# Two-layer hybrid encoder: inner matrices without a zero fill, queries and keys copied out ahead of the rotary, first scan tables and lambda factors moved

## The chip, the cores and the metric

One core of a Trainium2 chip. The metric is the device time of one execution in microseconds. TensorE (PE) multiplies, VectorE (DVE), ScalarE (ACT) and GpSimd (POOL) do the elementwise work, SyncE (SP) issues most transfers. Matmul results stand in PSUM, eight banks of 128 partitions by 512 floats; GpSimd works on SBUF only.

## The reference

```python
for layer in range(2):
    xn = rms_norm(x, norm_mix[layer]);  proj = xn @ w_in[layer]        # 256 x 1024 @ 1024 x 4096
    q, k, v, u, gates = split(proj)                                     # 512, 512, 512, 512, 2048 columns
    q, k = rotary(q), rotary(k)                                         # x1*cos - x2*sin, x2*cos + x1*sin
    lam = exp(sum(lp[0]*lp[1])) - exp(sum(lp[2]*lp[3])) + lam_init
    a = rms_norm(diff_attention(q, k, v, lam), attn_subln) * (1 - lam_init)
    s = gelu(s5_bidirectional(u, ...))                                  # complex diagonal scan, both directions
    s = s * sigmoid(s @ w_glu[layer])
    x = x + (g0 * (a @ w_branch[0]) + g1 * (s @ w_branch[1])) @ w_out[layer]
    x = x + (swiglu if layer == 0 else top-2-of-8 expert swiglu)(rms_norm(x, norm_ffn[layer]))
return rms_norm(x, norm_final)
```

The batch is 1, the sequence 256 tokens, the width 1024. All is in float32.

## The kernel before

Each large product is computed from split operands: ScalarE copies a 128 x 2048 tile of weights to `hi` (rounded, L1175), VectorE computes `lo` as the rest (L1568), and TensorE adds three products per 128 rows (L641, `three`). A layer's mixer has 25 such tiles, t + 0 to t + 24. The input projection takes tiles 0 to 15, two per group of 512 columns, in the order u, v, q, k and four gate groups; the four gate groups are interleaved with the attention and scan loop of eight turns. The 256 tokens are two halves `th`, each with its own accumulation bank `PJ[th]`.

The order of the work is written out by hand for every engine, with semaphores between them; there is no scheduler. The parts around the change:

- **Rotary** (VectorE, `rotary`). It waits for tiles 4 and 5 (queries) or 6 and 7 (keys), and per half multiplies `PJ[th]` with the cosines (L1621) and with the sines in two 256-wide pieces (L1624), both scaled by the inverse norm in the same operation, into the scratch `areg`. Then it releases the bank and adds both (L1629) to `qk`. In layer 0 the query rotary stands between `input_power(3)` and the split of tile 7, the key rotary before the splits of tiles 8 and 9.
- **Inner matrices** (TensorE, `inner`). A first matmul per bank writes 448 columns of zeros over the whole bank `PY` (the identity against a column of zeros), and then the diagonal `kdiag` and the 16-row products of `bbar` and `cblk` accumulate on it. ScalarE copies the result to `kc` (L1276), and SyncE moves pieces of it to `cbm` in 16 transfers (`inner_moves`, L554).
- **B transposed** (TensorE and ScalarE). Eight turns of transposes through two banks, evacuated by ScalarE (L1213) in the order 6, 7, 0, 1, 2, 3, 4, 5. After the turn g == 1 ScalarE makes the scan tables of turn 0 (`scan_tables(l, 0)`: L1284, then L1290), which wait for GpSimd's phase products (`wtab_half`, L2166 and L2167).
- **GpSimd** (layer 0): powers of C (`c_chain`, L430 to L436), phasors (L451 to L472), phase products (L410, L2166, L2167), then one `turn_forward` per turn (L2185 to L2192), whose states TensorE takes in `s5_out`. In layer 1 the powers and phasors are made long before.
- **VectorE before the loop**: `rotated(l, 0)` (L1642 to L1645) and `scanned(l, 0)` (L1655), then in layer 0 the lambda factors (L1791 to L1795), which wait for an exp by ScalarE (L1352); then eight turns with the row maximum (L1701) first.
- **TensorE in the loop**: scores, the scan's inputs (`s5_in`), scores, the transposed weights (`weights_t`, L804), half a gate projection, and `s5_out`.

Of the kernel before, what the change touches and what calls it, by code (L numbers as in the profile page):

```python
# [18 lines left out]
P = 128  # L19
# [3 lines left out]
HEADS, HD = 4, 64  # L23
# [6 lines left out]
PAIRS, GC, NS = 16, 16, 64  # L30
# [10 lines left out]
T_MIX = (0, T_MIX1)  # L41

C_ID, C_TRI, C_ONE, C_IOTA, C_SEL, C_COS, C_SIN = 0, 128, 256, 384, 512, 640, 768
# [80 lines left out]
def build(nc, x, norm_mix, w_in, attn_lambda, attn_subln, ssm_lam_re, ssm_lam_im, ssm_log_dt, ssm_b_re, ssm_b_im,  # L124
# [3 lines left out]
    ACT, ALU, AX = mybir.ActivationFunctionType, mybir.AluOpType, mybir.AxisListType  # L128
    MUL, ADD, SUB = ALU.mult, ALU.add, ALU.subtract
    ctx = ExitStack()  # L130
    with ctx:
# [15 lines left out]
        qk = sb("qk", [P, 2, TH, WA])  # L147
# [150 lines left out]
        def col(i, n=1):  # L298
            return small[:, i:i + n]
# [50 lines left out]
        def place_of(l, name):  # L350

            return W_IN_ORDER[l].index(name)
# [10 lines left out]
        def use(l, i):  # L363

            return PJ_PER_LAYER * l + i

        def pj_read(l, i):

            return (PJ_PER_LAYER - 2) * l + i + 1
# [269 lines left out]
        def _(pe):  # L639
            def mm(o, a, b, start, stop):  # L640
                return pe.matmul(o, a, b, start=start, stop=stop)  # L641
# [94 lines left out]
            def inner(l):  # L736

                if l == 0:
                    pe.wait_ge(loads, 16)
                pe.wait_ge(b_part, l + 1)  # L740
                for bank in PY:
                    mm(bank[:, 0:448], ident, cst[:, C_TRI:C_TRI + 1].broadcast_to([P, 448]), True, False)
                pe.wait_ge(kdiag_ready, l + 1)
                pe.wait_ge(c_ready, l + 1)
                for b, bank in enumerate(PY):
                    for half in range(2):
                        for g in range(2):
                            k = slice(64 * g, 64 * g + GC)
                            o = bank[64 * g + 32 * half:64 * g + 32 * half + GC, 0:448].rearrange("p (q c) -> p q c", q=4)
                            q0 = 8 * half + 4 * b  # L750
                            mm(o[:, :, 3 * GC:4 * GC], ident[k, k], kdiag[k, q0:q0 + 4, :], False, False)
                    for i in range(4):
                        for d in range(2):
                            c0 = 112 * i + (0 if d else 3 * GC)
                            for r in range(2):
                                for half in range(2):
                                    for g in range(2):
                                        q, rows, r0 = 8 * half + 4 * b + i, slice(64 * g, 64 * g + 64), 64 * g + 32 * half
                                        m = mm(bank[r0:r0 + GC, c0:c0 + 64], bbar[rows, r, q, d, :],
                                               cblk[rows, r, q, 4 * d:4 * d + 4, :].rearrange("p i h -> p (i h)"),  # L760
                                               False, i == 3 and d == 1 and r == 1)
                    m.then_inc(kc_full, 1)

            def channels(l):
# [403 lines left out]
        def _(act):  # L1168
# [12 lines left out]
            def split_static(t):  # L1181
                s = raw_slot(t)
                split(t, raw_full[s], 32 * (raw_uses(s, t) + 1), raw[:, s, :], t % SPLITS, t >= SPLITS)
# [115 lines left out]
            def mixer(l):  # L1299
# [34 lines left out]
                    evac((l, "u", g), ut4[:, 8 * g:8 * g + 8, :].rearrange("p q c -> p (q c)"))  # L1334
                split_static(t + 6)
                split_static(t + 7)
                split_static(t + 8)
                for i in range(t + 9, loop_tile(l) + 2):
                    split_static(i)
                for th in range(TH):  # L1340
                    evac_heads(l, "q", th, q_t)
                inner_copies(l)
# [2 lines left out]
                bflat = area(0, 4096)  # L1345
                for g in B_TURNS:
                    evac((l, "b", g), bflat[:, g * 512:(g + 1) * 512])
                    if g == 1:
                        scan_tables(l, 0)
                if l == 0:  # L1350
                    act.wait_ge(lam_ready, 1)
                    act.activation(col(LEXP, 4), col(LSUM, 4), ACT.Exp).then_inc(lam_exp, 1)  # L1352
                for s in range(8):
                    if s < 7:
                        scan_tables(l, s + 1)
# [206 lines left out]
        def _(dve):  # L1562
# [48 lines left out]
            def rotary(l, name, dst):  # L1611
                i = place_of(l, name)

                cos_t, sin_t = (cst[:, c:c + 128].rearrange("p (t c) -> p t c", t=2) for c in (C_COS, C_SIN))
                for th in range(TH):
                    if th == 0:
                        dve.wait_ge(pj0_full, use(l, i) + 1)
                    else:
                        dve.wait_ge(tile_used, T_MIX[l] + 2 * i + 2)
                    src = PJ[th][:, :]  # L1620
                    own.step(stt(a_flat[:, 0:512].rearrange("p (h c) -> p h c", c=HD), src.rearrange("p (h c) -> p h c", c=HD),  # L1621
                                 col(RI + th), cos_t[:, th, :].unsqueeze(1).broadcast_to([P, 8, HD]), MUL, MUL))
                    for a in range(2):
                        m = stt(a_flat[:, 512:1024].rearrange("p (h a c) -> p h a c", a=2, c=32)[:, :, a, :],  # L1624
                                src.rearrange("p (h a c) -> p h a c", a=2, c=32)[:, :, 1 - a, :], col(RI + th),
                                sin_t[:, th, 32 * a:32 * (a + 1)].unsqueeze(1).broadcast_to([P, 8, 32]), MUL, MUL)
                    m.then_inc(pj_free[th], 1)
                    dve.wait_ge(pj_free[th], pj_read(l, i))
                    tt(dst[:, th, :], a_flat[:, 0:512], a_flat[:, 512:1024], ADD).then_inc(rot_ready, 1)  # L1629
                    dve.wait_ge(rot_ready, 4 * l + (0 if name == "q" else 2) + th + 1)  # L1630

            def rotated(l, m):
# [108 lines left out]
            def mixer(l):  # L1741
# [36 lines left out]
                else:  # L1778
# [4 lines left out]
                    split_static(t + 8)  # L1783
                    split_static(t + 9)
                    rotary(l, "k", qk[:, 1, :, :])
                rotated(l, 0)
                scanned(l, 0)
                if l == 0:
                    dve.wait_ge(lam_exp, 1)
                    le = col(LEXP, 4).rearrange("p (l a) -> p l a", l=2)  # L1790
                    own.step(tt(col(NLAM, 2), le[:, :, 1], le[:, :, 0], SUB))  # L1791
                    for i in range(2):
                        lam_init = 0.8 - 0.6 * math.exp(-0.3 * i)
                        own.step(ts(col(NLAM + i), col(NLAM + i), -lam_init, None, ADD))
                        own.step(ts(subln[:, i, :], subln[:, i, :], 1.0 - lam_init, None, MUL))  # L1795
                for s in range(8):
                    row_max(l, s)
                    if s in LOOP_PROJ[l]:
                        split_static(loop_proj(l, s)[0] + 2)
                    softmax_factors(l, s)  # L1800
                    if s < 7:
                        rotated(l, s + 1)
                    weights(l, s)
                    if s < 7:
                        scanned(l, s + 1)
# [483 lines left out]
```

## Time and profile before

| | us |
|---|---|
| median of 3 runs | 1460.94 |
| lowest and highest | 1459.9, 1468.07 |
| span of the profiled execution | 1459.0 |
| PE busy | 1395.9 (96%) |
| DVE busy | 1129.3 (77%) |
| ACT busy | 893.5 (61%) |
| POOL busy | 350.5 (24%) |

The span runs from the first to the last instruction of the profiled execution; the times of the runs contain what lies around it, and the median is 1.94 us above it. The busy shares are means over stages: layer 0's mixer takes the first 264 us, the dense FFN runs up to about 438 us, layer 1's mixer up to about 640 us, and the experts take the rest. GpSimd's share stands almost all in the two mixers.

### The profile page before, as it was taken

Reading aid. Unit: us, or ns where it says so; the run is one execution under the profiler, and the core shown is the slowest. Engines: PE = TensorE matmul, PEld = TensorE weight load, DVE = VectorE, ACT = ScalarE, POOL = GpSimd, SP = SyncE. Lnnn points to the kernel's source line nnn. Section 1 sums busy time; section 2 is a strip of 40 time slices with the busy share of each in tenths; the row PEclk is TensorE's granted clock in tenths of the full one; section 3 lists DMA queues with packets and bytes.
Section 4 is the critical chain, followed back from the end, with each engine's and each line's share of the span. In section 5 each row is a group of like instructions: output and inputs, shape, how many; then the busy total and the mean of one; then the engine's idle time right before and its main releaser. Section 6 shows DMA issues by size and latency. Waiting matters only on the chain.

```text
span 1459.0 us, 23545 instructions
## 1 busy us (share of the span) xinstructions
PE 1395.9 (96%) x8569; PEld 1141.5 (78%) x8569; DVE 1129.3 (77%) x1036; ACT 893.5 (61%) x913; POOL 350.5 (24%) x428
## 2 busy tenths in 40 slices
PE   5989999999999999999999999999999999999997
PEld 4778777788877787777888888878888888788885
DVE  6967667655555577677889889898888898988886
ACT  4445555544345455555777777777777777777775
POOL 3888715998000187000000000000000000000000
PEclk9999999999999999998999999999999999999998
DMA  9433354565655332685999999999999999999981
GB/s 243 144 104 116 120 170 145 188 200 176 198 177 165 107 117 88 247 310 207 368 370 355 357 370 352 354 371 348 368 357 358 369 350 364 362 349 335 388 292 29
DMA packets 193075, 378.85 MB, mean 260 GB/s; under 512 B 17777, under 2 KB 57073, under 8 KB 192882
## 3 DMA queue, kind: packets, MB, share of 16 engines
q1 hardware_dynamic: 188256, 367.51, 71.8%
q0 software_dynamic: 2608, 7.87, 2.0%
q10 hardware_dynamic: 2146, 2.59, 0.6%
q8 instruction: 42, 0.69, 0.2%
q14 instruction: 23, 0.19, 0.0%
HBM read 374.78 MB, written 2.10 MB: 258 GB/s over the span
## 4 chain that ended last, share of the span: by engine, by line
PE 82%; DVE 7%; ACT 5%; issue 2%; DMA 1%; POOL 1%; SPq 0%; ACTq 0%; POOLq 0%; DVEq 0%
PE bank L641 79%; DVE lo L1568 4%; ACT hi L1175 3%; PE bank L1063 1%; PE bank L659 1%; DMA raw<-in_ssm_c_im_dram 1%; DMA raw<-in_w_in_dram 1%; ACT at_hi L1494 1%; POOL raw L2185 1%; POOL raw L2129 0%; PE bank L1044 0%; DVE raw L1678 0%; DVE bank L1680 0%; PE bank L967 0%; ACT at_hi L1478 0%
## 5 line engine op out<-in xcount | busy, mean ns | idle before, releaser
L1568 DVE TENSOR_TENSOR lo<-raw,hi 128x2048 fp32r<-128x2048 f32 x347 | 802.7, 2325 | 174.0 <-ACT hi L1175 173.8
L1175 ACT ACTIVATE hi<-raw 128x2048 fp32r<-128x2048 f32 x347 | 662.9, 1916 | 192.7 <-PE bank L641 191.7
L641 PE MATMUL bank<-hi,at_hi 128*128 128x512 f32 x1280 | 511.7, 400 | 16.1 <-DVE lo L1568 5.4
L641 PE MATMUL bank<-hi,at_lo 128*128 128x512 f32 x1280 | 500.9, 391 | 0.0
L641 PE MATMUL bank<-lo,at_hi 128*128 128x512 f32 x1280 | 499.9, 391 | 0.0
L641 PEld LDWEIGHTS bank<-hi,at_hi 128*128 128x128 f32 x1280 | 241.4, 189 | 71.1 <-DVE lo L1568 13.9
L641 PEld LDWEIGHTS bank<-hi,at_lo 128*128 128x128 f32 x1280 | 240.9, 188 | 52.2
L641 PEld LDWEIGHTS bank<-lo,at_hi 128*128 128x128 f32 x1280 | 241.6, 189 | 47.0
L641 PE MATMUL bank<-hi,ht_hi 128*128 128x512 f32 x440 | 172.1, 391 | 7.3 <-DVE lo L1568 4.7
L2232 POOL DMA_INDIRECT qk<-xn_rows,slot_row x7 | 18.7, 2670 | 651.9 <-DVE slot_row L2079 473.7
L641 PE MATMUL bank<-hi,ht_lo 128*128 128x512 f32 x440 | 171.4, 389 | 0.0
L641 PE MATMUL bank<-lo,ht_hi 128*128 128x512 f32 x440 | 171.2, 389 | 0.0
L641 PEld LDWEIGHTS bank<-hi,ht_hi 128*128 128x128 f32 x440 | 82.6, 188 | 27.4 <-issue 7.4
L641 PEld LDWEIGHTS bank<-hi,ht_lo 128*128 128x128 f32 x440 | 82.6, 188 | 17.3
L641 PEld LDWEIGHTS bank<-lo,ht_hi 128*128 128x128 f32 x440 | 82.6, 188 | 17.0
L1487 ACT ACTIVATE ht_hi<-bank 128x512 fp32r<-128x512 f32 (+1 forms) x48 | 27.1, 564 | 66.9 <-PE bank L1063 66.9
L2185 POOL TENSOR_TENSOR raw<-raw 128x256 f32<-128x256 f32 x64 | 50.9, 826 | 21.2 <-ACT raw L1290 7.9
L641 PEld LDWEIGHTS bank<-raw 64*64 64x64 f32 (+1 forms) x1664 | 43.8, 122 | 14.4 <-issue 6.3
L641 PE MATMUL bank<-raw 64*64 64x64 f32 (+1 forms) x1664 | 49.2, 220 | 6.0 <-POOL raw L2192 4.0
L430 POOL TENSOR_TENSOR raw<-raw,par 128x512 f32<-128x512 f32 (+2 forms) x24 | 29.8, 1260 | 62.5 <-ACT raw L1266 62.0
L1187 ACT ACTIVATE at_hi<-bank 128x512 fp32r<-128x512 f32 x32 | 17.6, 596 | 41.9 <-PE bank L659 41.8
L1483 ACT ACTIVATE vreg<-bank 128x512 f32<-128x512 f32 (+1 forms) x48 | 27.1, 565 | 25.1 <-PE bank L641 25.1
(285 smaller groups left out, 1149.6 us busy)
## 6 DMA issues: line engine op xcount, KB each, us to landing
raw<-in_moe_w_dram SPq DMA_DIRECT2D x528, 512.0 KB, 5.6
raw<-in_ffn_w_dram SPq DMA_DIRECT2D x66, 512.0 KB, 4.3
raw<-in_w_in_dram SPq DMA_DIRECT2D x64, 512.0 KB, 4.6
raw<-in_w_branch_dram SPq DMA_DIRECT2D x16, 512.0 KB, 4.1
raw<-in_w_out_dram SPq DMA_DIRECT2D x16, 512.0 KB, 6.5
raw<-in_w_glu_dram SPq DMA_DIRECT2D x4, 512.0 KB, 4.3
xres<-in_x_dram SPq DMA_DIRECT2D x2, 512.0 KB, 6.2
raw<-in_ssm_c_re_dram POOLq DMA_DIRECT2D x4, 256.0 KB, 6.5
```

What stands on the lines that cost most here:

```text
L430: tt(t1[:, r, q0:q1], source(r, q0, q1), num(re, q0, q1), MUL)
L641: return pe.matmul(o, a, b, start=start, stop=stop)
L659: last = pe.transpose(bank[:, i * rows:(i + 1) * rows], src, ident[0:rows, 0:rows])
L1063: m = pe.transpose(TR[0][:, f * P:(f + 1) * P], v_flat[:, f * P:(f + 1) * P], ident)
L1175: act.activation(hi[:, slot, :], src, ACT.Copy).then_inc(hi_ready, 1)
L1187: act.activation(at_hi[:, k0:k0 + kn, c0:c0 + P], bank[:, 0:kn * P].rearrange("p (k c) -> p k c", k=kn), ACT.Copy, scale=scale).then_inc(a ...
L1483: act.activation(v_flat[:, 0:h_width(c)], PJ[0][:, 0:h_width(c)], ACT.Silu).then_inc(g_ready, 1)
L1487: act.activation(ht_rows_hi[:, 0:h_width(c) // P, :], TR[0][:, 0:h_width(c)].rearrange("p (f s) -> p f s", s=P), ACT.Copy).then_inc(ht_hi_ ...
L1494: m = act.activation(at_hi[:, 4 * n:4 * n + 4, P:2 * P], PY[n][:, :].rearrange("p (k c) -> p k c", k=4), ACT.Copy, scale=place_gate)
L1568: tt(lo[:, slot, :], src, hi[:, slot, :].bitcast(f32), SUB).then_inc(lo_ready, 1)
L2185: last = tt(dst, src[:, :, :, d, :], w[:, r:r + 1, :, d, :].broadcast_to([P, 2, 2, 64]), MUL)
L2232: pool.indirect_dma_start(xg, None, xn_rows[:, :], bass.IndirectOffsetOnAxis(ap=slot_row[:, 0:1], axis=0)).then_inc(xg_in, 16)
```

## The change

1. `inner`: the two zero-filling matmuls of each layer go. The `kdiag` matmuls of each bank (four, one for each 32-partition group) start the accumulation in its place, and the products accumulate after them without a start.
2. `rotary`: ScalarE copies each half of q and k from `PJ[th]` to `qk`, scaled by the inverse norm, and releases the bank. VectorE multiplies and adds from there with plain `tensor_tensor` operations, in place. The copies stand in ScalarE's order after the split of tile 7 (q) and after that of tile 9 (k).
3. The scan tables of turn 0 in layer 0 are made after all eight evacuations of B; in layer 1 they stay after the fourth.
4. The exp of the lambda factors (layer 0) moves from after B to before the evacuation of the query transposes, and the factors themselves from after `scanned(0, 0)` to before `rotated(0, 0)`.

```diff
@@ inner @@
                 pe.wait_ge(b_part, l + 1)
-                for bank in PY:
-                    mm(bank[:, 0:448], ident, cst[:, C_TRI:C_TRI + 1].broadcast_to([P, 448]), True, False)
                 pe.wait_ge(kdiag_ready, l + 1)
...
-                            mm(o[:, :, 3 * GC:4 * GC], ident[k, k], kdiag[k, q0:q0 + 4, :], False, False)
+                            pe.matmul(o[:, :, 3 * GC:4 * GC], ident[k, k], kdiag[k, q0:q0 + 4, :], start=True, stop=False,
+                                      skip_group_check=True)
...
@@ scalar mixer @@
                 split_static(t + 7)
+                from_pj(l, place_of(l, "q"), t + 5, lambda th: qk[:, 0, th, :], ACT.Copy, inverse)
                 split_static(t + 8)
                 for i in range(t + 9, loop_tile(l) + 2):
                     split_static(i)
+                from_pj(l, place_of(l, "k"), t + 7, lambda th: qk[:, 1, th, :], ACT.Copy, inverse)
+                if l == 0:
+                    act.wait_ge(lam_ready, 1)
+                    act.activation(col(LEXP, 4), col(LSUM, 4), ACT.Exp).then_inc(lam_exp, 1)
...
-                    if g == 1:
+                    if g == 1 and l == 1:
                         scan_tables(l, 0)
                 if l == 0:
-                    act.wait_ge(lam_ready, 1)
-                    act.activation(col(LEXP, 4), col(LSUM, 4), ACT.Exp).then_inc(lam_exp, 1)
+                    scan_tables(l, 0)
@@ rotary @@
-                    if th == 0:
-                        dve.wait_ge(pj0_full, use(l, i) + 1)
-                    else:
-                        dve.wait_ge(tile_used, T_MIX[l] + 2 * i + 2)
-                    src = PJ[th][:, :]
-                    own.step(stt(a_flat[:, 0:512]..., src..., col(RI + th), cos_t[:, th, :]..., MUL, MUL))
+                    dve.wait_ge(pj_free[th], pj_read(l, i))
+                    src = dst[:, th, :]
+                    tt(a_flat[:, 0:512]..., src..., cos_t[:, th, :]..., MUL)
                     for a in range(2):
-                        m = stt(..., src[1 - a]..., col(RI + th), sin_t[:, th, 32 * a:32 * (a + 1)]..., MUL, MUL)
-                    m.then_inc(pj_free[th], 1)
-                    dve.wait_ge(pj_free[th], pj_read(l, i))
-                    tt(dst[:, th, :], a_flat[:, 0:512], a_flat[:, 512:1024], ADD).then_inc(rot_ready, 1)
+                        m = tt(..., src[1 - a]..., sin_t[:, th, 32 * a:32 * (a + 1)]..., MUL)
+                    own.step(m)
+                    tt(src, a_flat[:, 0:512], a_flat[:, 512:1024], ADD).then_inc(rot_ready, 1)
@@ vector mixer @@
-                rotated(l, 0)
-                scanned(l, 0)
                 if l == 0:
                     dve.wait_ge(lam_exp, 1)
...
+                rotated(l, 0)
+                scanned(l, 0)
```

## Rows read from the trace of the kernel before

**Rows 1.** The page's head.

```profile
span 1459.0 us, 23545 instructions
```

**Rows 2.** Chain that ended last, layer 0: start us, us, what.

```profile
71.83 2.30 DVE lo L1568
...
95.97 2.17 issue
```

**Rows 3.** Instructions by line, rotary: duration in ns min/median/max, first and last start.

```profile
L1621 DVE SCALAR_TENSOR_TENSOR areg<-bank,small,cst x8: 746/751/752, 65.6 to 489.5; 128x512 f32<-128x512 f32 x8
...
L1624 DVE SCALAR_TENSOR_TENSOR areg<-bank,small,cst x16: 474/480/486, 66.4 to 490.7; 128x256 f32<-128x256 f32 x16
...
L1629 DVE TENSOR_TENSOR qk<-areg x8: 692/692/1551, 67.3 to 491.2; 128x512 f32<-128x512 f32 x8
```

**Rows 4.** Timeline of VectorE, layer 0: start us, us (merged from first to last), operation.

```profile
67.28 1.55 DVE L1629 TENSOR_TENSOR qk<-areg 128x512 f32<-128x512 f32 x1
...
83.18 1.10 DVE L1629 TENSOR_TENSOR qk<-areg 128x512 f32<-128x512 f32 x1
...
84.31 4.89 DVE L1568 TENSOR_TENSOR lo<-raw,hi 128x2048 fp32r<-128x2048 f32 x2
```

**Rows 5.** Timeline of GpSimd, layer 0, the same stretch.

```profile
66.21 2.07 POOL L432 TENSOR_TENSOR raw<-raw,par 128x512 f32<-128x512 f32 x2
68.36 1.63 POOL L435 TENSOR_TENSOR raw<-raw 128x512 f32<-128x512 f32 x1
69.96 1.29 POOL L436 TENSOR_TENSOR raw<-raw 128x512 f32<-128x512 f32 x1
...
71.92 2.36 POOL L452 TENSOR_TENSOR raw<-par 128x64 f32<-128x64 f32 x1
...
75.53 0.31 POOL L452 TENSOR_TENSOR raw<-php_last 128x64 f32<-128x64 f32 x1
...
97.49 0.45 POOL L2167 TENSOR_TENSOR raw<-php_last 128x128 f32<-128x128 f32 x1
```

**Rows 6.** Timeline of TensorE, layer 0: in brackets idle time and releaser.

```profile
67.39 0.47 PE L641 MATMUL bank<-hi,at_hi 128*128 128x512 f32 x1 [2.00 <-DVE areg L1624]
...
80.62 1.67 PE L641 MATMUL bank<-cst 128*128 128x448 f32 x4
82.23 0.30 PE L641 MATMUL bank<-raw,cst 16*16 16x64 f32 x8
...
101.84 0.67 PE L641 MATMUL bank<-qk,ureg 64*128 64x256 f32 x2 [0.74 <-issue]
...
109.81 1.38 PE L641 MATMUL bank<-raw 64*64 64x64 f32 x40
...
119.74 1.38 PE L641 MATMUL bank<-raw 64*64 64x64 f32 x40
```

**Rows 7.** Timeline of ScalarE, layer 0.

```profile
49.63 0.69 ACT L1224 ACTIVATE vreg<-bank,small 128x512 f32<-128x512 f32 x1 [0.74 <-PE bank L641]
...
97.97 0.51 ACT L1290 ACTIVATE raw<-raw 128x128 f32<-128x128 f32 x2 [3.12 <-POOL raw L2167]
```

**Rows 8.** Timelines around the loop's start, layer 0: SyncE, VectorE, GpSimd.

```profile
91.11 12.58 SPq L554 DMA_DIRECT2D raw<-areg  x16
...
100.91 1.26 DVE L1655 TENSOR_TENSOR_SCAN raw<-raw,bank 128x256 f32<-128x256 f32 x2
...
105.38 0.69 DVE L1701 TENSOR_REDUCE small<-bank 128x2 f32<-128x512 f32 x1
...
106.03 2.83 POOL L2192 TENSOR_TENSOR raw<-raw 128x256 f32<-128x256 f32 x1
```

**Rows 9.** Timelines of TensorE and GpSimd, layer 1.

```profile
477.11 0.47 PE L641 MATMUL bank<-hi,at_hi 128*128 128x512 f32 x1 [0.62 <-DVE areg L1624]
...
488.99 1.67 PE L641 MATMUL bank<-cst 128*128 128x448 f32 x4
...
506.59 0.10 POOL L2178 MEMSET raw<- 128x4 f32 x1 [147.41 <-DVE raw L1655]
```

More of the change, by code:

```diff
@@ L758, in inner @@
                                         q, rows, r0 = 8 * half + 4 * b + i, slice(64 * g, 64 * g + 64), 64 * g + 32 * half
-                                        m = mm(bank[r0:r0 + GC, c0:c0 + 64], bbar[rows, r, q, d, :],
-                                               cblk[rows, r, q, 4 * d:4 * d + 4, :].rearrange("p i h -> p (i h)"),
-                                               False, i == 3 and d == 1 and r == 1)
+                                        m = pe.matmul(bank[r0:r0 + GC, c0:c0 + 64], bbar[rows, r, q, d, :],
+                                                      cblk[rows, r, q, 4 * d:4 * d + 4, :].rearrange("p i h -> p (i h)"),
+                                                      start=False, stop=i == 3 and d == 1 and r == 1, skip_group_check=True)
                     m.then_inc(kc_full, 1)
@@ L1615, in rotary @@
                 for th in range(TH):
-                    if th == 0:
-                        dve.wait_ge(pj0_full, use(l, i) + 1)
-                    else:
-                        dve.wait_ge(tile_used, T_MIX[l] + 2 * i + 2)
-                    src = PJ[th][:, :]
-                    own.step(stt(a_flat[:, 0:512].rearrange("p (h c) -> p h c", c=HD), src.rearrange("p (h c) -> p h c", c=HD),
-                                 col(RI + th), cos_t[:, th, :].unsqueeze(1).broadcast_to([P, 8, HD]), MUL, MUL))
-                    for a in range(2):
-                        m = stt(a_flat[:, 512:1024].rearrange("p (h a c) -> p h a c", a=2, c=32)[:, :, a, :],
-                                src.rearrange("p (h a c) -> p h a c", a=2, c=32)[:, :, 1 - a, :], col(RI + th),
-                                sin_t[:, th, 32 * a:32 * (a + 1)].unsqueeze(1).broadcast_to([P, 8, 32]), MUL, MUL)
-                    m.then_inc(pj_free[th], 1)
-                    dve.wait_ge(pj_free[th], pj_read(l, i))
-                    tt(dst[:, th, :], a_flat[:, 0:512], a_flat[:, 512:1024], ADD).then_inc(rot_ready, 1)
+                    dve.wait_ge(pj_free[th], pj_read(l, i))
+                    src = dst[:, th, :]
+                    tt(a_flat[:, 0:512].rearrange("p (h c) -> p h c", c=HD), src.rearrange("p (h c) -> p h c", c=HD),
+                       cos_t[:, th, :].unsqueeze(1).broadcast_to([P, 8, HD]), MUL)
+                    for a in range(2):
+                        m = tt(a_flat[:, 512:1024].rearrange("p (h a c) -> p h a c", a=2, c=32)[:, :, a, :],
+                               src.rearrange("p (h a c) -> p h a c", a=2, c=32)[:, :, 1 - a, :],
+                               sin_t[:, th, 32 * a:32 * (a + 1)].unsqueeze(1).broadcast_to([P, 8, 32]), MUL)
+                    own.step(m)
+                    tt(src, a_flat[:, 0:512], a_flat[:, 512:1024], ADD).then_inc(rot_ready, 1)
                     dve.wait_ge(rot_ready, 4 * l + (0 if name == "q" else 2) + th + 1)
```

## The prediction

> **What bounds the kernel now.** I read the page first (its span is the sum everything below is made against [rows 1]), then the chain of work that ended last, then the timeline of one engine at a time through the two places that the diff touches: 55 to 112 us in layer 0, and 465 to 510 us in layer 1. Over the whole run the chain is TensorE's, so a microsecond counts only where TensorE stands still or where it does the removed work. In layer 0 the chain is VectorE's up to 74.1 us: query rotary, then the split of tile 7, and only then can TensorE start its last key tile [rows 2]. After that it is TensorE's, with a 2.17 us hole named "issue" in the middle of the transposes of B [rows 2]. In layer 1 TensorE is hardly held up: 0.62 us before the key tiles [rows 9].
>
> **A rule seen in the rows.** VectorE's operations that read PSUM never vary: the two multiplies of the rotary take 746 to 752 and 474 to 486 ns in all uses. The closing add, whose two inputs are both in SBUF, takes 692 ns in most and 1551 in the worst [rows 3]. The slow ones lie where GpSimd works. At 67.28 the add takes 1.55 us: GpSimd's second operation of the pair that began at 66.21 ends at 68.28, and then 0.6 us are left for the add. GpSimd's next operation then takes 1.63 us, where the equal one behind it takes 1.29 [rows 4, 5]. It is the same the other way round: a 64-element GpSimd operation that takes 0.31 us elsewhere took 2.36 us under VectorE's split of tile 7 [rows 2, 5]. In the pair of splits at 84.31 one GpSimd operation slips in ahead of each: 4.89 us for two, where one alone takes 2.30 [rows 2, 4]. So I read it as an exclusive turn: an operation of VectorE with two SBUF inputs and one of GpSimd never run together, and they alternate when both have work queued.
>
> The Trainium skill, page "SBUF — State Buffer", section "Who interferes with whom", says just this: VectorE with two SBUF inputs against a GpSimd operation that reads SBUF, and whichever starts later fully blocks. The trace agrees (1.55 against 0.69 us). By that rule this change moves eight operations of each layer into the contended class; without it the sum for layer 0 would be that of the first rival below.
>
> **Layer 0, rotary of the queries.** What it removes: the rotary's multiplies no longer read PJ, so ScalarE copies two banks out (0.69 us each [rows 7]), ScalarE being idle then. Tile 5 ends at 65.4 (2.00 us of idle time before 67.39 [rows 6]), so PJ[1] is free at about 66.1 instead of when the rotary lets go; TensorE's key tile 6 starts near 65.3 and not 67.39. That gain of 2.1 us is worth nothing as such, since tile 7 waits for the split, and the split is behind the rotary in VectorE's order. What it adds: the cosine multiply, the two sine multiplies and the add all have two SBUF inputs now, 8 operations instead of 2. Alone they would take 0.62, 0.38, 0.42 and 0.62 us (from the 692 ns add, and 692 less the 751 - 480 between the two widths [rows 3], less the overlap of neighbours): 4.1 us for both halves. But GpSimd is at its C powers: between them it puts the rest of one operation (0.7), then two of 1.04, two of 1.29 (the pair at 66.21, and the ones at 68.36 and 69.96, free of their own waits [rows 5]), then three short ones of 0.2 to 0.55. With the waits inside each half that is 10.3 us, so the rotary runs 65.6 to 75.9. Before it ran to 71.83, with two waits only. I take a difference of **+3.8 us**: stepping both orders with the same rule gave that, and the split of tile 7 ends at 77.9, not 74.1. Bounds: below, -2.0 (no contention: 4.4 us of rotary in place of 6.25); above, +5.
>
> **Layer 0, TensorE up to the loop.** Tile 7 runs 78.0 to 83.7, the query transposes to 84.6. The zero fill of the two banks is gone: four matmuls from 80.62 to the next at 82.23, **-1.6 us** [rows 6]. Its cover was none, it stood in TensorE's order with both waits behind it already met. The kdiag matmuls that start the groups instead cost what they did. The inner matrices end near 90.1. The key rotary meets GpSimd's short operations (0.2 to 0.4 us each, eight times) and ends at about 89.5 instead of 84.28 [rows 4], just in time for the key transposes. So TensorE is 3.8 - 1.6 = **+2.2 us** late as it enters the transposes of B.
>
> There the first scan tables no longer stand in ScalarE's order between two evacuations of B; ScalarE had waited 3.12 us there for GpSimd [rows 7]. How much TensorE gets back has two ends: 2.17 us if the hole is that wait, nothing if it is TensorE's own, and the profile puts it to "issue" and inside a turn whose bank was already free. TensorE could start the loop between 101.8 (as now [rows 6]) and 104.0.
>
> **Layer 0, the loop's first turn.** GpSimd is what is late next. Each of VectorE's added operations also pushes it: six more in the queries and six in the keys, each 0.4 to 0.6 us, and the shifted splits block it as before. It finished the phase products of the first tables at 97.94 [rows 5]; I get +5.2 from the same stepping, and 0.3 more since the lambda factors, now ahead, also read SBUF: 103.5. ScalarE's copies follow (0.5; evacuations and the exp with its table load are out of the way, the exp being moved to an idle ScalarE near 85), VectorE's turn and scan (3.7) end at 107.7 instead of 102.17, and GpSimd's own turn forward, 6.7 us with one block by a split, gives the first states at 114.4 where it gave them at 108.86 [rows 8]. TensorE wants them at 109.81 [rows 6]; the slack before was 0.95 us. So TensorE waits until 114.4, **+4.6 us** for layer 0, whatever the hole above does. Moving the lambda factors and their wait ahead takes away the 3.2 us between the scan's end and the first row maximum [rows 8], so that comes at 107.7 against 105.38: 2.3 us later for a TensorE that is 4.6 late. It costs and gains nothing. A turn of TensorE takes 9.93 us [rows 6]; GpSimd's 6.7 and its phase products fit inside, so the delay stays and does not grow.
>
> **Layer 1.** GpSimd is idle from before the rotaries until 506.59 [rows 9], so nothing contends. TensorE gets PJ 0.62 us earlier and loses the zero fill, 1.67 us [rows 9]: **-2.3 us**. VectorE's rotary is 0.2 us shorter per half and stays covered. The scan tables stay where they were in layer 1.
>
> **Sum.** 1459.0 + 4.6 - 2.3 = 1461.3 us of span; the median of the runs stands 1.94 us above this profiled span, which gives 1463.2. FFN and experts only start later by that much.
>
> **The rivals.** 0.5% here is 7.3 us, about what a measurement of this kernel can tell from none.
>
> *The added SBUF reads are free* (faster). Speaks for it: the sine multiplies are small and broadcast. Against: [rows 4, 5]. Then split 7 ends at 72.1 (-2.0), the fill goes (-1.6), GpSimd is early and the hole may close (0 to -2.2): -3.6 to -5.8 in layer 0, with layer 1 -5.9 to -8.1: 1455 to 1452.8. Chance 0.15; it would also need TensorE's next waits to follow.
>
> *Contention costs TensorE only what the rotary adds; GpSimd keeps its slack* (no change to the eye). GpSimd's end moves by 3 us and not 5.5, first states at 112, PE +2.2: 1461. Chance 0.25.
>
> *The edge moves of the inner matrices become late* (slower). SyncE issues their 16 transfers over 12.6 us from 91.11 [rows 8], after the load that waits for tile 9's split. That split goes from 89.2 to 94.4, so the last is issued near 109 and lands around 112. It decides only if first states come before that or if the issue stretches by over 2.5 us; with 4 us more, TensorE's first output turn starts at 118: 1467. Chance 0.12.
>
> Forecast itself 0.48.
>
> **Range and chances.** The likeliest case alone spans 1461 to 1466. Free reads at their end reach 1453, the late moves 1467, and both tails beyond are thin, so 80% lies in 1456 to 1467.5. Faster by over 0.5% (under 1453.6) needs the free reads with the hole closed: 0.06. Slower by over 0.5% (over 1468.2) needs late moves on top of the forecast: 0.07. Within: 0.87.
>
> **What would show it.** In the timeline of VectorE, rotary operations in layer 0 of uneven length, up to 1.7 us, and even ones in layer 1; the split of tile 7 at 75.9 and not before 72; GpSimd's last phase product of the first table near 103.5; TensorE idle before the first output turn of layer 0, released by GpSimd; the zero fill gone from both layers; layer 1's stretch from tile 6 to the loop 2.3 us shorter. Wrong if the rotary in layer 0 is over in 5 us, or if TensorE meets the first states without a wait.

## The result, and the profile after

The changed kernel takes 1470.71 us (median of 14 runs, 1464.88 to 1474.48), beside 1461.97 (14 runs, 1459.68 to 1470.67) of the kernel before on the same chip: ratio 1.0043, 95% interval 1.0028 to 1.0059. By this ratio, which is not the quotient of the two medians, the change costs 6.3 us (4.1 to 8.6), where I had 2.3 us; the median lies 3.2 us above my range, though the ratio itself stays within 0.5%. The profiled execution is the slowest of the 14, and the profile before was one of the faster ones, so the two traces differ by 13.6 us of span. The places are to be read from them, the sizes with that in mind.

The page's head and its row of the granted clock, against [rows 1]:

```profile
span 1472.6 us, 23537 instructions
...
PEclk9988999999999999998999999999999999999999
```

Eight matmuls and their eight weight loads are gone (the zero fill) and eight copies of ScalarE are new, which makes eight instructions fewer. The clock row has two slices of 8, from 74 to 147 us, where that of before has 9. The rotary, grouped by line, against [rows 3]: durations min/median/max in ns, then first and last start.

```profile
L1621 DVE TENSOR_TENSOR areg<-qk,cst x8: 684/692/1674, 65.9 to 504.0; 128x512 f32<-128x512 f32 x8
...
L1624 DVE TENSOR_TENSOR areg<-qk,cst x16: 416/445/1498, 67.2 to 504.9; 128x256 f32<-128x256 f32 x16
...
L1628 DVE TENSOR_TENSOR qk<-areg x8: 691/691/1432, 69.7 to 505.4; 128x512 f32<-128x512 f32 x8
```

All three lines now have the long durations that only the add had. VectorE's timeline in layer 0, against [rows 4]:

```profile
65.89 1.35 DVE L1621 TENSOR_TENSOR areg<-qk,cst 128x512 f32<-128x512 f32 x1
67.16 2.48 DVE L1624 TENSOR_TENSOR areg<-qk,cst 128x256 f32<-128x256 f32 x2
69.68 1.43 DVE L1628 TENSOR_TENSOR qk<-areg 128x512 f32<-128x512 f32 x1
71.14 1.67 DVE L1621 TENSOR_TENSOR areg<-qk,cst 128x512 f32<-128x512 f32 x1
...
75.44 2.29 DVE L1571 TENSOR_TENSOR lo<-raw,hi 128x2048 fp32r<-128x2048 f32 x1
```

The query rotary takes 9.55 us instead of 6.25, it starts 0.3 us later, and the split of tile 7 starts at 75.44 (I had 75.9). What then happens to TensorE stands in the chain that ended last, against [rows 2]: start, us, what.

```profile
75.44 2.30 DVE lo L1571
77.79 8.12 PE bank L641 x24
...
99.72 3.62 issue
103.34 4.33 PE bank L641 x88
108.41 8.08 PE bank L641 x60
116.48 2.92 issue
119.40 5.73 PE bank L641 x76
...
125.75 11.97 PE bank L641 x104
```

Set beside the same marks of before (both from TensorE's timeline and the chain):

| TensorE in layer 0 | before | after | late by |
|---|---|---|---|
| tile 7 starts | 74.17 | 77.79 | 3.6 |
| query transposes (tile 7 took 5.7, then 8.1) | 79.75 | 85.75 | 6.0 |
| inner matrices | 82.23 | 86.71 | 4.5 |
| transposes of B | 89.22 | 93.61 | 4.4 |
| after the hole in B (2.17, then 3.62) | 98.14 | 103.34 | 5.2 |
| loop starts | 101.84 | 108.41 | 6.6 |
| first output turn (2.92 of waiting) | 109.81 | 119.40 | 9.6 |
| second output turn | 119.74 | 134.01 | 14.3 |
| layer 1, transposes of B | 497.49 | 510.95 | 13.5 |

From the second output turn on, the delay stays between 13.5 and 15.7 us; the one stretch in which it shrinks by more than 2 us is layer 1. The clock is the part that was not in my sum. The windows view of the changed kernel (window, its length, busy time and count of PE, PEld, DVE, ACT and POOL, granted clock, DMA share, GB/s):

```profile
74.00:84.00 10.00, 6.21 (x17) 4.96 (x18) 8.52 (x16) 1.15 (x2) 9.13 (x23) 0.66 0.33 106
...
104.00:114.00 10.00, 9.26 (x130) 7.84 (x129) 4.83 (x8) 5.67 (x13) 1.99 (x8) 0.86 0.15 28
...
124.00:134.00 10.00, 10.00 (x32) 7.54 (x32) 6.95 (x11) 2.80 (x9) 7.77 (x12) 0.66 0.32 107
```

and of the kernel before:

```profile
74.00:84.00 10.00, 9.82 (x156) 7.68 (x160) 9.66 (x21) 2.70 (x3) 8.91 (x27) 1.00 0.32 106
...
124.00:134.00 10.00, 10.00 (x108) 8.09 (x107) 7.60 (x12) 4.98 (x14) 8.82 (x13) 1.00 0.33 107
```

1.00 is the level of 2.4 GHz; a mean of 0.66 is a stretch partly at 1.2. In the last window TensorE is busy throughout in both kernels. Their counts, 32 against 108, can't be compared, because the small matmuls of an output turn (72 of them) fall into the window of before alone. What the clock does is seen in the large ones: at 126 us those of 128x512 start 0.43 us apart, at 112 us, at full clock, 0.23. Each of the three low stretches between 74 and 134 us follows a standstill: 5.34 us before tile 7, 3.62 us in the middle of B, 2.92 us before the first output turn.

Who was last before that output turn? ScalarE, VectorE and GpSimd in their timelines, the bracket being idle time and what ended it:

```profile
104.89 0.60 ACT L1212 ACTIVATE raw<-bank 128x512 f32<-128x512 f32 x1 [4.77 <-PE bank L641]
...
107.71 0.60 ACT L1212 ACTIVATE raw<-bank 128x512 f32<-128x512 f32 x1 [0.52 <-PE bank L641]
108.20 0.40 ACT L1283 ACTIVATE raw<-par 128x252 f32<-128x252 f32 x1
108.51 0.50 ACT L1289 ACTIVATE raw<-raw 128x128 f32<-128x128 f32 x2
```

```profile
101.86 0.45 POOL L2166 TENSOR_TENSOR raw<-php_last 128x128 f32<-128x128 f32 x1
...
112.81 0.10 POOL L2177 MEMSET raw<- 128x4 f32 x1 [8.01 <-DVE raw L1654]
```

```profile
111.43 1.26 DVE L1654 TENSOR_TENSOR_SCAN raw<-raw,bank 128x256 f32<-128x256 f32 x2
```

GpSimd finished the phase products of the first tables at 102.3, earlier than my 103.5, and after those of the next tables, from 104.8, it stood idle for 8.01 us. ScalarE starts the tables at 108.2, right behind the last evacuation of B. So the first states are not late because of GpSimd, as I had written, but because the tables now stand in ScalarE's order behind all of TensorE's transposes of B, and TensorE is late there.

### The profile page after: what moved, and what is told of

Same layout as the page of the kernel before. It is cut to its first block, busy times and chain, and to the rows that moved or that the text cites. A ratio compares the mean times of both kernels' runs of the same rounds, so it can differ in the third digit from the quotient of the medians.

```text
span 1472.6 us, 23537 instructions
## 1 busy us (share of the span) xinstructions
PE 1403.3 (95%) x8561; PEld 1149.0 (78%) x8561; DVE 1128.9 (77%) x1036; ACT 898.2 (61%) x921; POOL 354.3 (24%) x428
## 4 chain that ended last, share of the span: by engine, by line
PE 82%; DVE 7%; ACT 5%; issue 3%; DMA 1%; POOL 1%; SPq 0%; ACTq 0%; POOLq 0%; DVEq 0%
PE bank L641 78%; DVE lo L1571 4%; ACT hi L1174 2%; PE bank L1062 1%; PE bank L659 1%; DMA raw<-in_ssm_c_im_dram 1%; DMA raw<-in_w_in_dram 1%; ACT at_hi L1497 1%; POOL raw L2184 1%; PE bank L758 1%; POOL raw L2128 0%; PE bank L1043 0%; DVE raw L1677 0%; DVE bank L1679 0%; PE bank L966 0%
## 5 line engine op out<-in xcount | busy, mean ns | idle before, releaser
L641 PEld LDWEIGHTS bank<-raw 64*64 64x64 f32 x1152 | 37.5, 139 | 14.8 <-issue 7.3
L641 PE MATMUL bank<-raw 64*64 64x64 f32 x1152 | 42.0, 225 | 6.8 <-POOL raw L2191 3.8
L1700 DVE TENSOR_REDUCE small<-bank 128x2 f32<-128x512 f32 x16 | 11.0, 690 | 38.2 <-PE bank L641 38.2
```

## The experiments

Each ratio is to the kernel before on the same chip, with its 95% interval; the three groups of runs had their own runs of the kernel before (medians 1461.81, 1463.64 and 1462.31). The ratio is not the quotient of the medians. Readings from a trace are of one execution, and for three runs it is not a typical one: with parts 3 and 4 alone it was the fastest of 11, with the fill removed and the moves first the second fastest of 12, and with the operand in PSUM the slowest of 10.

### One part at a time

**The fill alone removed**, from the kernel before:

```diff
-                for bank in PY:
-                    mm(bank[:, 0:448], ident, cst[:, C_TRI:C_TRI + 1].broadcast_to([P, 448]), True, False)
+                # kdiag matmuls with start=True, products with start=False, as in the change
```

> The kernel before with part 1 of the change alone (no zero fill in the inner matrices). Theory C (the loss is the rotary's: its reads of SBUF alternate with GpSimd in layer 0, VectorE's split and GpSimd's states come late, and TensorE's clock falls in the idle time) and rival M (the loss comes from the moved scan tables) both expect 1.6 us less per layer, 3.3 us less in all (ratio 0.9977). A third view, that the fill lay in time TensorE spends waiting anyway for GpSimd before the loop of layer 0, expects 1.6 us less, all of it in layer 1, and the loop of layer 0 to begin at 101.8 us as before.

Measured: 1.0026 (1.0007 to 1.0044), 1466.96 us. Taking work away from TensorE made it slower, which none of the three views had. Its chain:

```profile
98.83 3.68 PE bank L641 x64
...
103.26 15.50 PE bank L641 x136
```

TensorE comes to the transposes of B at 87.78, 1.4 us earlier, and gains nothing by it: the loop starts at 103.26, after 101.84 before. A hole of 2.25 us stays, and then TensorE waits another 1.79 us for ScalarE, which waits for GpSimd's products before it makes the tables in the middle of B (98.83). The 136 matmuls of the first turn take 15.50 us instead of 11.68, at a granted clock of 0.81 from 104 to 124. So the removed work of layer 0 became standstill, and the clock took 3.8 us more.

**The rotary alone** (part 2, with ScalarE's copies):

```diff
+                from_pj(l, place_of(l, "q"), t + 5, lambda th: qk[:, 0, th, :], ACT.Copy, inverse)
...
-                    own.step(stt(a_flat[:, 0:512]..., src..., col(RI + th), cos_t..., MUL, MUL))
+                    tt(a_flat[:, 0:512]..., src..., cos_t..., MUL)
...
```

> The kernel before with part 2 alone (ScalarE copies q and k out, VectorE's rotary reads SBUF). Theory C: 5 to 11 us more; in layer 0 the split of tile 7 ends near 78 us, TensorE idles 5 us before tile 7, the granted clock falls there, and that tile takes about 8 us instead of 5.7. Rival M: 0.6 to 2 us less, since VectorE's rotary gets shorter and PJ is free sooner.

Measured: 0.9995 (0.9975 to 1.0015), 1462.89 us. Its chain:

```profile
77.29 8.61 PE bank L641 x24
...
106.01 11.68 PE bank L641 x136
```

Tile 7 is 3.1 us late and runs slow (8.61 us), so TensorE comes to the loop at 106.01, 4.2 late. But it then finds the states ready, since the tables were made early; there is no second standstill, and no second low clock. What theory C expected at tile 7 is there, the 5 to 11 us in the time are not.

**Tables and lambda factors alone** (parts 3 and 4):

```diff
-                    if g == 1:
+                    if g == 1 and l == 1:
                         scan_tables(l, 0)
                 if l == 0:
...
+                    scan_tables(l, 0)
...
```

> The kernel before with parts 3 and 4 alone (first scan tables of layer 0 after all of B, exp and lambda factors ahead). Theory C: 0 to 2 us less; first row maximum near 103 us. Rival M: 4 to 8 us more, with first states of layer 0 late and TensorE waiting for them.

Measured: 1.0019 (1.0003 to 1.0035), 1465.15 us. Its chain:

```profile
100.70 8.03 PE bank L641 x60
108.73 2.97 issue
111.70 3.71 PE bank L641 x76
```

With a rotary as before and the loop 1.1 us early, since the holes in B are shorter (0.80 us in all, after 0.53 and 2.17), TensorE still waits 2.97 us for the first states. That wait comes with the table move. Rival M had the mechanism, and at 4 to 8 us too high a price; theory C had a gain. No low clock follows the wait in this trace, the fastest of the 11.

**The change, with the old rotary in layer 0:**

```diff
...
+                (rotary_bank if l == 0 else rotary_copied)(l, name, dst)
```

`rotary_bank` is the rotary of the kernel before, `rotary_copied` that of the change; ScalarE's copies stay in layer 1 alone.

> The changed kernel with the rotary of layer 0 as before (it reads the banks and scales by itself, no copies), layer 1 as changed. Theory C: faster than before by 3.5 to 6 us (2.3 in layer 1, the rest in layer 0), and 10 us or more faster than the changed kernel; no idle time of 5 us before tile 7. Rival M: still slower than before by 2 us or more.

Measured: 1.0009 (0.9990 to 1.0028), 1463.87 us. Tile 7 starts at 73.65 and takes 5.78 us. The hole in B is 3.07 us, longer than before and without any contention, and the loop's first turn takes 14.81 us at a low clock in place of a wait. Keeping this one part back recovers most of the loss (0.34 of 0.43%). The gain over the kernel before, which theory C expected, is not there.

### Which link of the chain

**The change, edge moves before the loads of tiles 11 and 12.** SyncE issues the 16 small transfers of `kc` two tiles earlier in its order.

```diff
-                        if t == loop_tile(l) + 5:
+                        if t == loop_tile(l) + 3:
                             inner_moves(l)
```

> The changed kernel with SyncE's 16 moves of the inner matrices issued before the loads of tiles 11 and 12 instead of behind them. Theory H (TensorE's hole of 3.6 us in the transposes of B is its instruction block, whose load stands behind 2 MB of weights): the hole is under 1 us, the loop of layer 0 begins 3 us or more sooner, 3 to 6 us faster than the changed kernel. Rival (the hole is a wait for ScalarE or GpSimd): hole unchanged, time unchanged. Rival (moves late): TensorE waits less for the first states if the moves were what it waited for, with the hole unchanged.

Measured: 1.0006 (0.9990 to 1.0022), 1466.07 us. The chain has no hole in B any more:

```profile
92.15 8.68 PE bank L641 x288
...
101.56 8.04 PE bank L641 x60
109.60 2.96 issue
```

The reason stands in the DMA view. Of the change from 93.6 to 100.8 us, the queues (packets, MB, share of 16 engines):

```profile
q1 hardware_dynamic: 1194, 1.96, 83.1%
```

and of this kernel, the equal stretch of 7.2 us from 92.6 to 99.8:

```profile
q1 hardware_dynamic: 1431, 0.33, 25.2%
q8 instruction: 2, 0.03, 1.8%
```

Queue q8 brings the blocks of instructions, 16 KB each. In the transposes of B, made of many small matmuls, a block arrives every 3.5 to 4 us; here it got two, in the change none, while the weights of tiles 11 and 12 were filling the DMA engines. The change's next block began at 100.89 and the hole ended at 103.34; before it was 95.84 and 98.14, with the old rotary 94.13 and 96.55, with the operand in PSUM 93.37 and 95.75. In these four kernels the hole ends 2.3 to 2.45 us behind the begin of a block. So the "issue" in the middle of B is TensorE waiting for instructions behind weights. The wait for the states is unchanged at 2.96, though the edge moves were issued at 91.42 and not at 95.39: it was not them that the first output turn waited for.

**The change, with the tables back after the fourth evacuation:**

```diff
-                    if g == 1 and l == 1:
+                    if g == 1:
                         scan_tables(l, 0)
-                if l == 0:
-                    scan_tables(l, 0)
```

> The changed kernel with the first scan tables of layer 0 back after the fourth evacuation of B. Theory S (the tables behind all evacuations make VectorE's scan and GpSimd's first states late): tables follow GpSimd's phase products at 102.3 us, first states 4 to 6 us sooner, 3 to 5 us faster than the changed kernel. Rival G (GpSimd is the bound, as in the prediction): less than 1 us.

Measured: 1.0009 (0.9990 to 1.0029), 1464.75 us. VectorE's first scan in this kernel:

```profile
104.20 1.26 DVE L1652 TENSOR_TENSOR_SCAN raw<-raw,bank 128x256 f32<-128x256 f32 x2
```

It starts 7.2 us earlier than in the change, and TensorE does not wait for the states at all, though GpSimd and the rotary are as contended as in the change. That refutes my step: in the change GpSimd was not what set the first output turn. (TensorE still has a low clock in the first turn, 15.52 us, behind the standstill that the tables bring into B: ScalarE makes them from 101.26, when GpSimd's products are done, and TensorE waits 2.20 us for the evacuation behind them.)

**The change, with the fill kept:**

> The changed kernel with the zero fill kept. Theory K (without the fill TensorE's clock falls for 10 us or more before or in the loop of layer 0, or the instruction blocks fall on a worse place): 2 to 6 us faster than the changed kernel although TensorE does 3.3 us more work, clock at its high level from 90 to 130 us. Rival (the fill is plain work, worth 1.6 us a layer): 3.3 us slower than the changed kernel.

Measured: 1.0042 (1.0021 to 1.0062), 1472.14 us: no difference from the change. The edit is the first diff above, reversed. Both expectations missed: the 1.6 us of each layer are neither saved nor paid. Its loop starts at 105.47, even before the change's 108.41, since its hole in B is smaller (1.07 us); the wait of 2.92 and the low clock after it (6.59 and 11.02 us for what takes 3.71 and 9.56) are the same.

**The fill removed and the moves first**, from the kernel before (both diffs above):

> The kernel before without the zero fill and with the moves issued before the loads of tiles 11 and 12. Without the fill alone the time was 1.0026 of before, with a hole of 2.25 us and 13.7 us of low clock behind it. Theory H: hole under 1 us, no low clock at the start of the loop, ratio 0.996 to 0.999. Theory K in its strong form (the dense fill itself keeps the clock up): low clock at the loop's start again, ratio 1.001 or more.

Measured: 1.0013 (0.9994 to 1.0031), 1467.58 us. The hole is gone, and TensorE then waits 6.40 us for ScalarE, which waits for GpSimd's products; the loop starts at 105.76. Removing one wait made the next one larger: with the tables in the middle of B, GpSimd's products bound B. The traced execution took 1460.9 us at a mean granted clock of 0.990; nine of the twelve took 1467.1 to 1469.0 at 0.982 to 0.985. So most of them had more low clock than the traced one, and the ratio is theory K's; whether it fell at the loop's start, as K has it, no trace shows. Nor is it shown that the fill itself kept the clock up: the long standstill in B could do the same.

### The two mechanisms by themselves

**Contention: the same multiplies with an operand in PSUM.** In layer 0 ScalarE scales the bank in place, and the plain multiplies read it there; only the add has two SBUF inputs.

```diff
+                    act.activation(PJ[th][:, :], PJ[th][:, :], ACT.Copy, scale=inverse(th)).then_inc(pj_scaled, 1)
-                    src = dst[:, th, :]
+                    src = PJ[th][:, :]
```

> The changed kernel, but in layer 0 ScalarE scales q and k in place in their banks and VectorE's three multiplies read the banks; the same operations, with one SBUF input instead of two. Theory P (two SBUF inputs against GpSimd): the multiplies of layer 0 take 0.7 and 0.9 us for the pair, as in layer 1, and the split of tile 7 begins 2.5 to 3.5 us after where the query rotary could start plus 5 us, not 9.5. Rival (the operations are slow for another reason, their form or the cosines' broadcast): they keep 1.35 and 2.5 us.

Measured: 0.9992 (0.9972 to 1.0012), 1463.88 us. VectorE's timeline:

```profile
65.15 0.69 DVE L1641 TENSOR_TENSOR areg<-bank,cst 128x512 f32<-128x512 f32 x1
65.76 0.74 DVE L1644 TENSOR_TENSOR areg<-bank,cst 128x256 f32<-128x256 f32 x2
66.54 0.98 DVE L1652 TENSOR_TENSOR qk<-areg 128x512 f32<-128x512 f32 x1
...
70.04 3.27 DVE L1587 TENSOR_TENSOR lo<-raw,hi 128x2048 fp32r<-128x2048 f32 x1
```

The same operations on the same data, beside the same GpSimd work, take 0.69 us (one of 128x512) and 0.74 (a pair of 128x256) from PSUM where they took 1.35 and 2.48 from SBUF. The rotary takes 4.9 us in all, and the split of tile 7 begins 5.4 us earlier. The wait of 2.94 us for the states stays.

**Clock: TensorE kept busy.** The change, with dummy matmuls of 128 x 512 in the two standstills of layer 0, 20 before tile 7 and 10 before the first output turn. They do only what fills the time.

```diff
+                    if l == 0 and i == 3:
+                        bank = open_turn((l, "q", 0))
+                        for _ in range(20):
+                            mm(bank[:, :], at_hi[:, 0, 0:P], at_hi[:, 0:2, :].rearrange("p k s -> p (k s)"), True, True)
```

> The changed kernel with dense matmuls of no use in the two waits of layer 0 (20 of 512 columns between tiles 6 and 7, 10 ahead of the first output turn), which end before the waits would. Theory K (idle time pulls TensorE's clock down, and the low stretch behind it costs half its length): tile 7 takes 5.7 us instead of 8.1 and the first two turns 9.9 each; low stretches near 76 and 120 us gone; 3 to 8 us faster than the changed kernel (ratio to before 0.999 to 1.002). Rival (the loss is in the waits alone): unchanged, 1.004.

Measured: 0.9999 (0.9982 to 1.0016), 1464.27 us. TensorE's timeline, then the windows:

```profile
71.83 4.70 PE L641 MATMUL bank<-at_hi 128*128 128x512 f32 x20
77.61 0.50 PE L641 MATMUL bank<-hi,at_hi 128*128 128x512 f32 x1 [1.08 <-DVE lo L1579]
```

```profile
74.00:84.00 10.00, 8.92 (x44) 7.09 (x42) 9.77 (x19) 1.28 (x3) 9.23 (x21) 1.00 0.31 106
...
124.00:134.00 10.00, 10.00 (x115) 8.10 (x112) 7.99 (x13) 5.10 (x15) 8.49 (x12) 1.00 0.36 121
```

Tile 7 still starts late (77.61), the contention is untouched, and work was added; yet the clock stays at 1.00 in both windows, the chain beyond is at full pace, and 0.44% come back. It is not the traced execution alone: the twelve runs had mean granted clocks of 0.987 to 0.991, the 14 of the change 0.980 to 0.987. The low clock was caused by the standstills. (Its hole in B is short too, 0.36 us after 3.62, so not all of the gain need be the clock. And with B over that early, GpSimd's products, ready at 102.1, are what the tables wait for.)

### Two candidates

**Fill and rotary of layer 0 as before, layer 1 as changed, lambda factors ahead, tables of layer 0 after the sixth evacuation of B:**

```diff
-                    if g == 1:
+                    if g == (3 if l == 0 else 1):
                         scan_tables(l, 0)
```

> A candidate: fill and rotary of layer 0 as before, layer 1 as changed, lambda factors ahead, and the first scan tables of layer 0 after the sixth evacuation of B. Expected from the terms measured so far: 2.3 us less in layer 1 and about 1 less in layer 0, ratio 0.997 to 0.999. Rival: any reordering in layer 0 costs its gain again in states or clock, ratio 1.000 or more.

Measured: 0.9977 (0.9961 to 0.9992), 1459.15 us: faster than both kernels, by 3.4 us (1.2 to 5.7) than the one before. Its chain:

```profile
97.55 0.51 ACT raw L1292 x2
...
99.13 8.04 PE bank L641 x60
107.16 1.33 issue
108.49 3.71 PE bank L641 x76
```

After the sixth evacuation GpSimd's products are about ready (97.5), so neither ScalarE nor TensorE stands long: 1.33 us before the output turn, which comes at 108.49 and not 109.81. The dense FFN starts 1.2 us earlier than before, layer 1's transposes of B 3.2 us earlier, and the span is 3.1 us shorter.

**The kernel before, with parts 1 and 2 in layer 1 alone:**

> A candidate: the kernel before with parts 1 and 2 of the change in layer 1 alone. 2.3 us less in layer 1, ratio 0.998 to 0.999; no low clock in layer 1, since TensorE has no wait there that grows. Rival: without the fill layer 1 loses its gain in clock, ratio 1.000 or more.

Measured: 1.0005 (0.9985 to 1.0025), 1465.66 us; the expected gain did not show in the time. It is in the trace: from the start of the dense FFN to layer 1's transposes of B the kernel before takes 229.2 us, this one 227.3. But in its profile the loop of layer 0, whose code is that of the kernel before, takes 15.39 us for the turn that took 11.68, behind a loop start of 104.09. Its 12 runs lie from 1458.9 (mean granted clock 0.991) to 1467.9 (0.984), about as those of the kernel before (1459.0 to 1468.1): whether a low clock falls in layer 0 differs from one execution to the next, and covers the 2 us of layer 1.

## Why the prediction was wrong, step by step

- **Rotary of the queries, +3.8 us by contention: right.** +3.6 measured. (My own working, 10.3 us after 6.25, gives 4.05, and the change moves twelve multiplies of each layer into the contended class, six for the queries and six for the keys, where I wrote eight.) The PSUM variant shows that it is the second SBUF input and nothing else in the rotary. The rival of free reads is out.
- **Zero fill, -1.6 us: right where it stood, wrong as a gain.** The ledger has it (6.0 late becomes 4.5), but alone it made the kernel slower (1.0026), and kept it changed nothing (1.0042). Behind it wait instruction blocks and, with the tables in B, GpSimd.
- **The hole in B, "gives back 0 to 2.2": wrong in sign.** I named two owners, ScalarE's wait or TensorE itself. It was neither: the hole is an instruction block queued behind 2 MB of weights, and the new timing lengthened it by 1.4 us. The moves-first kernel removed it.
- **First states at 114.4 set by GpSimd, +4.6 for layer 0, "whatever the hole above does": the step that failed in the order of the work.** They came at 119.40, set by ScalarE's place in the order. I asked when GpSimd would be done (102.3, better than my 103.5) and took ScalarE's copies as prompt. But the copies stand behind TensorE's last transposes. In five kernels with the moved tables the first output turn comes 11.0 us behind the loop's start: 100.70 to 111.70 (parts 3 and 4 alone), 101.56 to 112.56 (moves first), 100.56 to 111.56 (PSUM rotary), 105.47 to 116.46 (fill kept), 108.41 to 119.40 (the change). TensorE's own work in between is 8.0. (With the old rotary in layer 0 a low clock stretched that work, and no wait was left.) So TensorE waits for a consequence of its own lateness: every delay up to the loop is carried on in full, plus 3.0, where the old order gave the states a date of their own and let TensorE be 4.2 us late for nothing (rotary alone).
- **No term for TensorE's clock: the missing term of the sum.** Tile 7 took 2.4 us more, the end of B 1.4, the first two turns 4.4 to 4.7: about 8.5 of the 14.3 us by which the second output turn is late. Tile 6 from 65.3 and tile 7 from 78.0, as I had them, mean a longer standstill between the two, and I costed it as the lateness alone. The filler shows the cause.
- **Late edge moves, the slower rival: not what happened** as I put it. They did shift from 91.11 [rows 8] to 95.39, but with the moves first they went out 4 us earlier and the wait stayed at 2.96: the first output turn waited for states. Their place in the order mattered in another way: behind the weights, they leave the instruction blocks no room.
- **GpSimd keeps its slack, the rival without a change to the eye: not what happened.** GpSimd's end moved by 4.4 us (97.94 to 102.31), between this rival's 3 and my 5.5, and it had slack left; but TensorE came to the loop 6.6 us late and not 2.2.
- **Layer 1, -2.3 us: right.** 15.66 late at the start of the dense FFN, 13.46 at layer 1's B. The wait of 0.62 us before the key tiles [rows 9] and the fill are gone. The chain there, with no standstill before the inner matrices:

```profile
469.80 33.25 PE bank L641 x265
...
510.95 8.79 PE bank L641 x288
```

My sum of 1461.3 had 4.6 - 2.3; the ratio says 6.3 us, with 2.2 given back by layer 1. So layer 0 costs about 8.5 us in a typical run, which is an estimate, and 15.7 up to the dense FFN in the profiled one, 1.6 of it in the FFN's first tile (7.32 us after 5.73).

The signs by which I wanted to know that I was right all came: uneven rotary operations, the split of tile 7 near 75.9, GpSimd's products near 103.5, a wait before the first output turn. The wait was there for another reason than mine. Only its date, 119.4 and not 114.4, and the clock tell the two apart.

The losses do not belong to single parts. Alone, the parts give -0.05%, +0.26% and +0.19%, which sums to 0.40%, close to the 0.43% of all together. Yet the rotary, which costs nothing alone, brings back 0.34 percentage points when it is undone, and the fill, which costs 0.26 alone, brings back 0.01. So the agreement of the sum looks like chance. Undoing any one link (old rotary, tables back, moves first, PSUM operand, filler) brings back 0.34 to 0.51 points. The likeliest reading, argued and not shown, is that each link either shortens a standstill, and with it the low clock behind it, or frees the states from TensorE's date; the intervals, each about 0.2 points to both sides, do not separate these five from one another.

The mean granted clock was read in every run, traced or not, and says more than the single traces. In 35 runs of the kernel before (those of the first group) it goes from 0.992 at 1459.0 us down to 0.982 at 1470.1, with a median of 0.989. So low stretches come and go in the kernel before too, and most of its spread goes with them. The 14 runs of the change lie at 0.980 to 0.987, with a median of 0.982. As an estimate, 0.007 less over 1460 us is up to 10 us of TensorE's time: the lower clock is large enough for the whole loss of a typical run.

Open: why the fill kept or removed makes no difference in the whole change, when its removal alone costs 0.26%; and when a standstill is followed by a low clock. That of 2.97 us in the run of parts 3 and 4 alone was not, and that of 2.92 in the change was. But the former trace is the fastest of its eleven runs (0.992), and the other ten have 0.985 to 0.989, so it may differ by execution and not by kernel; where their low stretches lie, no trace shows.

## What to carry to other kernels

Before an edit is costed, write down for each wait whether its date is set by another engine or by the waiting engine's own earlier work: a step moved behind the bottleneck's output turns slack into a fixed delay, and then every microsecond before it counts in full. Where TensorE bounds, price a longer standstill twice, as lateness and as the slower matmuls that may follow it (here up to 4.7 us); an edit that removes work ahead of a wait can lose by it. Where an operation of VectorE must run beside GpSimd's chain, try one of its operands in PSUM: here that brought a pair of 2.48 us down to 0.74. And before one trace is taken for the kernel, look where its execution lies among the runs, in time and in granted clock.

## What the runs showed of the hardware

- Plain VectorE multiplies with both inputs in SBUF, beside GpSimd's chain: 1.35 and 1.67 us for 128x512, 2.48 and 1.94 for a pair of 128x256. With one input in PSUM: 0.69 and 0.74, with all twelve of layer 0 within 2 ns (690 to 692) and 4 ns (411 to 415) of their kind.
- TensorE's granted clock fell to 1.2 GHz behind a standstill of 5.3 us in layer 0, and tile 7 took 8.1 us, not 5.7; 20 dummy matmuls in that gap kept it at 2.4 GHz. Behind waits of 2.9 us it fell in four traced kernels of five, and the first two turns took 4.3 to 4.7 us more. The Trainium skill ("TensorE: Matmul & The Clock Gate", section "HAM oscillation — how this bites in real kernels") warns of idle gaps between matmuls; the trace agrees.
- An instruction block of TensorE can queue behind weight traffic: holes of 2.2 to 3.6 us in a stretch of small matmuls, gone when the weights came later. The Trainium skill ("Runtime: NRT & Kernel Launch", section "Instruction fetch mechanics") calls the cost of crossing a block "mostly hidden"; here it is not hidden where some hundred matmuls of 64x64 run while the DMA engines are 83% busy, and the measurement decides.
